# Moving the small tensors of a hybrid decoder layer behind its weight ring in SBUF

## The chip, the cores and the metric

The kernel runs on one core of a Trainium2 chip. The metric is the device time of one execution in microseconds (us), lower is better, taken as the median of the runs.

## The reference

One decoder layer on x of 1024 tokens by 1024 features, in float32, then a last RMSNorm. What matters for the work:

```python
h = rmsnorm(x, norm_mix_g)
u_pool, q, k, v, f_logit, g_logit = split(h @ w_in)            # 1024 x 4104
y_pool = pool_mixer(u_pool, pool_w, pool_scale) @ w_pool_out   # windows 2, 4, 8, 16
y_fox = forgetting_attention(q, k, v, f_logit + b_forget) @ w_fox_out   # 8 heads of 64, causal
g_pool, g_fox = split(sigmoid(g_logit + b_gate))
x = x + (g_pool * y_pool + g_fox * y_fox) @ w_out
x = x + memory_cross_attention(rmsnorm(x), rmsnorm(mem), w_xq, w_xkv, w_xo)  # 256 memory tokens
gate, up = split(rmsnorm(x) @ w_ffn_in)                        # 1024 x 5632
x = x + (silu(gate) * up) @ w_ffn_out                          # 2816 x 1024
out = rmsnorm(x, norm_final_g)
```

## The kernel before

Every matrix product is done in three passes: each operand is split into a high part in the reduced format float32r and a low part, the rest. `mm3` (lines 1553 to 1555) multiplies high by low, high by high and low by high into one PSUM bank. Weights stream from HBM in chunks of 1024 columns per partition. SyncE loads a chunk into one of two buffers `w_raw` (line 420), ScalarE copies it to one of three `w_hi` (line 657), and VectorE, or GpSimd for seven chunks, subtracts to get `w_lo` (lines 1043 and 517). TensorE waits for `w_lo`. A chunk that is a block of 128 columns of a weight arrives in pieces of 512 bytes per row of the weight; `w_pool_out` comes in pieces of 1 KB.

The stages run in this order: norm and input projections, pooling mixer, attention, gates and `w_out`, cross attention, then the FFN. Both FFN products use seven block products in place of eight (Winograd's form of Strassen's method), so GpSimd forms sums of weight blocks (`w_sum`, lines 581 to 586) and of hidden blocks (`h_sum`), and the hidden values go out to HBM (`hs_dram`) and come back into the halves of `w_raw` (line 473). Activations are split as well, on the lines 668, 984 and 1054. All engines are tied by semaphores, with the order of each engine written out by hand. Nothing in that order depends on where a tensor lies.

What the change touches is where the tensors lie in SBUF. A tensor made by `keep` stays for the whole program. The allocator gives out each partition's bytes in the order of the calls and rounds each tensor up to 32 bytes. The first `keep` tensor begins at byte 8320. A tensor made by `place(name, kb, ...)` begins kb KiB above the end of all the `keep` tensors, and such tensors overlay each other in time. Here are the `keep` tensors:

- 17 small ones for statistics, biases and counts (`ss` to `x_inv`), 1440 bytes with rounding. Most of them are read as one column of 128x1: the sum of squares `ss` (34 columns, line 506), the rsqrt `rstd`, biases.
- `w_raw`, `w_hi`, `w_lo` (eight tensors of 4096 bytes) and `ident`, `ident_r`, `mask`, `mask_r` (512 bytes each), 34,816 bytes. They are called the ring below.

Everything else (`h_hi`, `u_sb`, `win`, `z_hi`, `xr`, `hf_hi`, `wq`, `s2_hi`, `t2_hi` and so on) is placed above. Most placed tiles start a whole number of KiB above the base. The exceptions are within tiles: `u_sb` has four rows of 16 + 1024 numbers (4160 bytes a row), and `win` has 16 numbers (64 bytes) of padding in front of 1024.

Of the kernel before, what the change touches and what calls it, by code (L numbers as in the profile page):

```python
# [16 lines left out]
F32R = mybir.dt.float32r  # L17
# [4 lines left out]
P = 128  # L22
# [20 lines left out]
RAWS, SLOTS = 2, 3  # L43
# [72 lines left out]
def build(nc, x, mem, norm_mix_g, w_in, b_forget, b_gate, pool_w, pool_scale, w_pool_out,  # L116
# [12 lines left out]
    with ctx:  # L129
        def keep(name, shape, dt=FP32):  # L130
            return ctx.enter_context(nc.sbuf_tensor(name, shape, dt))
# [6 lines left out]
                return st.enter_context(nc.sbuf_tensor(name, shape, dt))  # L138


        n_tiles = N_OUT + T
        ss = keep("ss", [P, n_tiles])
        ms = keep("ms", [P, n_tiles])
# [12 lines left out]
        x_nmax = keep("x_nmax", [P, XH, T])  # L156
        x_sum = keep("x_sum", [P, XH, T])
        x_inv = keep("x_inv", [P, XH, T])

        w_raw = [keep(f"w_raw{i}", [P, 1024]) for i in range(RAWS)]  # L160
        w_hi = [keep(f"w_hi{i}", [P, 1024], F32R) for i in range(SLOTS)]
        w_lo = [keep(f"w_lo{i}", [P, 1024], F32R) for i in range(SLOTS)]
        ident = keep("ident", [P, P])
        ident_r = keep("ident_r", [P, P], F32R)
        mask = keep("mask", [P, P])
        mask_r = keep("mask_r", [P, P], F32R)


        h_hi = place("h_hi", 0, [P, KD, S], F32R)
# [1942 lines left out]
```

## Time and profile before

| | us |
|---|---|
| median of 3 runs | 1521.78 |
| lowest and highest | 1520.59, 1523.24 |
| the profiled execution's own time | 1521.78 |
| its span, first to last instruction | 1519.9 |
| outside the span | 1.9 |

Mean granted clock of TensorE: 0.990 of full speed (core 0, the only one). The span is what the profile's views explain; the 1.9 us around it are in the time alone. TensorE is abbreviated PE, its weight loads PEld, VectorE DVE, ScalarE ACT, GpSimd POOL. A group line gives the line in the kernel, the engine, the operation, what is written and read, the shapes, a count, the busy time in us and the mean duration of one in ns.

### The profile page before, as it was taken

The page shows a single profiled execution, that of the slowest core. Times are in us where ns is not written, and L with a number is a line of the kernel's source. Part 1 is how long each engine was busy: PE and PEld are TensorE (multiplying, and loading weights), DVE is VectorE, ACT ScalarE, POOL GpSimd, SP SyncE. Part 2 cuts the span into 40 slices and gives each one's busy share as a digit, 9 for nine tenths or more (in the row PEclk, how much of TensorE's full clock was granted, in tenths as well). Part 3 has the DMA queues.
Part 4 walks back from the last instruction along what each step waited for, and adds up shares of the span by engine and source line. Part 5 has one row for each costly group of instructions (what it writes and reads, how often), then busy time and mean ns, then how long its engine had stood idle before and what let it go on. Part 6 is the DMA issues. An engine that isn't in the chain of part 4 may idle for free.

```text
span 1519.9 us, 18589 instructions
## 1 busy us (share of the span) xinstructions
PE 1466.1 (96%) x7268; PEld 1211.3 (80%) x7268; DVE 898.3 (59%) x1226; ACT 555.7 (37%) x987; POOL 377.9 (25%) x311
## 2 busy tenths in 40 slices
PE   5999999999999999999999799999999999999996
PEld 5778888788787888888877678888888888887785
DVE  4272522566665423327563866777677776878966
ACT  5224311656654322216451542222222222444344
POOL 4000000000000000105001654444444443448203
PEclk9999999999999999999999899999999999999998
DMA  7333355531110352513210223323332224883333
GB/s 183 54 48 56 72 82 83 98 57 22 49 29 29 73 80 83 222 51 105 67 42 28 111 70 104 105 104 104 104 104 104 104 104 152 304 285 84 104 97 132
DMA packets 103399, 147.79 MB, mean 97 GB/s; under 512 B 4744, under 2 KB 69768, under 8 KB 101904
## 3 DMA queue, kind: packets, MB, share of 16 engines
q1 hardware_dynamic: 94288, 117.72, 30.0%
q0 software_dynamic: 4464, 15.77, 2.9%
q10 hardware_dynamic: 4560, 13.11, 2.2%
q8 instruction: 58, 0.95, 0.2%
q14 instruction: 29, 0.24, 0.1%
HBM read 113.78 MB, written 32.80 MB: 96 GB/s over the span
## 4 chain that ended last, share of the span: by engine, by line
PE 89%; DVE 5%; POOL 2%; DMA 2%; ACT 1%; issue 1%; SPq 0%; POOLq 0%; DVEq 0%; ACTq 0%
PE ps L1553 27%; PE ps L1554 27%; PE ps L1555 27%; PE ps L1803 2%; PE ps L1752 2%; PE ps L1783 1%; DMA w_raw<-in_w_in 1%; DVE t_lo L1054 1%; PE ps L1784 1%; DVE s_lo L1054 1%; POOL w_lo L517 1%; POOL rstd L509 0%; PE ps L1560 0%; PE ps L1995 0%; DVE hf_lo_B L1054 0%
## 5 line engine op out<-in xcount | busy, mean ns | idle before, releaser
L1043 DVE TENSOR_TENSOR w_lo<-w_raw,w_hi 128x1024 fp32r<-128x1024 f32 (+1 forms) x58 | 70.5, 1216 | 232.2 <-ACT w_hi L657 230.3
L1553 PE MATMUL ps<-h_lo,w_hi 128*128 128x512 f32 (+1 forms) x456 | 181.3, 398 | 6.5 <-POOL w_lo L517 4.6
L1555 PE MATMUL ps<-h_hi,w_lo 128*128 128x512 f32 (+1 forms) x456 | 176.8, 388 | 0.0
L1554 PE MATMUL ps<-h_hi,w_hi 128*128 128x512 f32 (+1 forms) x456 | 176.5, 387 | 0.0
L657 ACT ACTIVATE w_hi<-w_raw 128x1024 fp32r<-128x1024 f32 (+1 forms) x66 | 69.4, 1051 | 286.4 <-PE ps L1555 270.7
L1553 PE MATMUL ps<-t_lo,s_hi 128*128 128x512 f32 x308 | 120.2, 390 | 2.3 <-DVE t_lo L1054 1.5
L1555 PE MATMUL ps<-t_hi,s_lo 128*128 128x512 f32 x308 | 119.9, 389 | 0.0
L1554 PE MATMUL ps<-t_hi,s_hi 128*128 128x512 f32 x308 | 119.9, 389 | 0.0
L1553 PEld LDWEIGHTS ps<-h_lo,w_hi 128*128 128x128 f32 x456 | 86.4, 190 | 23.3 <-POOL w_lo L517 4.8
L1555 PEld LDWEIGHTS ps<-h_hi,w_lo 128*128 128x128 f32 x456 | 86.3, 189 | 17.8
L1554 PEld LDWEIGHTS ps<-h_hi,w_hi 128*128 128x128 f32 x456 | 86.6, 190 | 15.5
L1054 DVE TENSOR_TENSOR s_lo<-w_raw,s_hi 128x512 fp32r<-128x512 f32 x77 | 68.0, 884 | 51.4 <-ACT s_hi L984 51.4
L984 ACT ACTIVATE s_hi<-w_raw 128x512 fp32r<-128x512 f32 x77 | 48.7, 632 | 126.9 <-PE ps L1555 104.4
L1553 PE MATMUL ps<-hf_lo_T,w_hi 128*128 128x512 f32 x212 | 82.5, 389 | 0.0
L1554 PE MATMUL ps<-hf_hi_T,w_hi 128*128 128x512 f32 x212 | 82.5, 389 | 0.0
L1555 PE MATMUL ps<-hf_hi_T,w_lo 128*128 128x512 f32 x212 | 82.5, 389 | 0.0
L998 ACT ACTIVATE p_sb<-ps 128x512 f32<-128x512 f32 x22 | 13.0, 598 | 188.7 <-PE ps L1555 188.7
L1054 DVE TENSOR_TENSOR t_lo<-wq_B,t_hi 128x512 fp32r<-128x512 f32 x77 | 73.5, 954 | 0.0
L1553 PE MATMUL ps<-hf_lo_B,w_hi 128*128 128x512 f32 x164 | 66.0, 402 | 5.6 <-DVE hf_lo_B L1054 5.6
L1553 PEld LDWEIGHTS ps<-t_lo,s_hi 128*128 128x128 f32 x308 | 57.8, 188 | 16.2 <-issue 4.2
L1555 PEld LDWEIGHTS ps<-t_hi,s_lo 128*128 128x128 f32 x308 | 57.8, 188 | 12.1
L1554 PEld LDWEIGHTS ps<-t_hi,s_hi 128*128 128x128 f32 x308 | 57.8, 188 | 11.7
(303 smaller groups left out, 3658.8 us busy)
## 6 DMA issues: line engine op xcount, KB each, us to landing
w_raw<-hs_dram SPq DMA_DIRECT2D x77, 256.0 KB, 2.8
w_raw<-in_w_in SPq DMA_DIRECT2D x33, 512.0 KB, 7.7
raw_p<-in_w_ffn_in SPq DMA_DIRECT2D x22, 512.0 KB, 4.6
w_raw<-in_w_ffn_in SPq DMA_DIRECT2D x22, 512.0 KB, 4.3
hs_dram<-h_sum SPq DMA_DIRECT2D x11, 1024.0 KB, 9.0
hs_dram<-hq SPq DMA_DIRECT2D x11, 768.0 KB, 7.1
wq_B<-in_w_ffn_out SPq DMA_DIRECT2D x8, 1024.0 KB, 8.2
x_in<-in_x SPq DMA_DIRECT2D x8, 512.0 KB, 10.1
```

Source lines behind the costliest of these rows:

```text
L517: nc.gpsimd.tensor_tensor(w_lo[n % SLOTS][:], w_raw[n % RAWS][:], w_hi[n % SLOTS][:].bitcast(FP32), ALU.subtract).then_inc(lo_ready, 1)
L657: nc.scalar.activation(w_hi[n % SLOTS][:, 0:w], w_raw[n % RAWS][:, 0:w], ACT.Copy).then_inc(hi_ready, 1)
L984: nc.scalar.activation(s2_hi[n % SLOTS2][:], s_raw(n % SLOTS2), ACT.Copy).then_inc(s_split_hi, 1)
L1043: nc.vector.tensor_tensor(w_lo[n % SLOTS][:, 0:w], w_raw[n % RAWS][:, 0:w], w_hi[n % SLOTS][:, 0:w].bitcast(FP32), ALU.subtract).then_inc( ...
L1054: nc.vector.tensor_tensor(out, a, hi.bitcast(FP32), ALU.subtract).then_inc(done, 1)
L1553: nc.tensor.matmul(dst, w_h, x_l, start=start, stop=False)
L1554: nc.tensor.matmul(dst, w_h, x_h, start=False, stop=False)
L1555: return nc.tensor.matmul(dst, w_l, x_h, start=False, stop=stop)
L1752: last = nc.tensor.transpose(ps[:, 4 + g % 2, tile_of(j - j0)], prob[v % 2][:, a, tile_of(j)], ident[:])
L1783: nc.tensor.matmul(dst, q1a[:, tile_of(i)], k1a[:, keys], start=True, stop=False)
L1784: last = nc.tensor.matmul(dst, q2a[:, tile_of(i)], k1a[:, keys], start=False, stop=not diagonal)
L1803: last = nc.tensor.matmul(ps[a * DH:(a + 1) * DH, 6, 0:P], v_sb[:, j, hc:hc + DH], prob_t[:, a, tile_of(j)], start=j == 0, stop=j == v % T)
```

## The change

The small tensors are allocated after the ring and no longer before it. A tensor of 32 bytes that nothing uses (`line_fill`) is put ahead of the ring, and another (`line_fill2`) behind the small tensors. No instruction is added, removed or reordered, and no DMA changes its shape.

```diff
--- before.py
+++ after.py
@@ -138,6 +138,14 @@
                 return st.enter_context(nc.sbuf_tensor(name, shape, dt))
 
 
+        keep("line_fill", [P, 8])
+        w_raw = [keep(f"w_raw{i}", [P, 1024]) for i in range(RAWS)]
+        w_hi = [keep(f"w_hi{i}", [P, 1024], F32R) for i in range(SLOTS)]
+        w_lo = [keep(f"w_lo{i}", [P, 1024], F32R) for i in range(SLOTS)]
+        ident = keep("ident", [P, P])
+        ident_r = keep("ident_r", [P, P], F32R)
+        mask = keep("mask", [P, P])
+        mask_r = keep("mask_r", [P, P], F32R)
         n_tiles = N_OUT + T
         ss = keep("ss", [P, n_tiles])
         ms = keep("ms", [P, n_tiles])
@@ -156,14 +164,7 @@
         x_nmax = keep("x_nmax", [P, XH, T])
         x_sum = keep("x_sum", [P, XH, T])
         x_inv = keep("x_inv", [P, XH, T])
-
-        w_raw = [keep(f"w_raw{i}", [P, 1024]) for i in range(RAWS)]
-        w_hi = [keep(f"w_hi{i}", [P, 1024], F32R) for i in range(SLOTS)]
-        w_lo = [keep(f"w_lo{i}", [P, 1024], F32R) for i in range(SLOTS)]
-        ident = keep("ident", [P, P])
-        ident_r = keep("ident_r", [P, P], F32R)
-        mask = keep("mask", [P, P])
-        mask_r = keep("mask_r", [P, P], F32R)
+        keep("line_fill2", [P, 8])
 
 
         h_hi = place("h_hi", 0, [P, KD, S], F32R)
```

The addresses follow from the sizes, as the byte in each partition:

| | before | after | moved by |
|---|---|---|---|
| `line_fill` | none | 8320 | |
| small tensors, from `ss` | 8320 | 43168 | +34848 |
| ring, from `w_raw0` | 9760 | 8352 | -1408 |
| `line_fill2` | none | 44608 | |
| base of the placed tensors | 44576 | 44640 | +64 |

## Rows read from the trace of the kernel before

**Rows 1.** The page: the span, and busy time of each engine.
```profile
span 1519.9 us, 18589 instructions
...
PE 1466.1 (96%) x7268; PEld 1211.3 (80%) x7268; DVE 898.3 (59%) x1226; ACT 555.7 (37%) x987; POOL 377.9 (25%) x311
```

**Rows 2.** The page, chain that ended last: shares of the span by engine and by line.
```profile
PE 89%; DVE 5%; POOL 2%; DMA 2%; ACT 1%; issue 1%; SPq 0%; POOLq 0%; DVEq 0%; ACTq 0%
PE ps L1553 27%; PE ps L1554 27%; PE ps L1555 27%; PE ps L1803 2%; PE ps L1752 2%; PE ps L1783 1%; DMA w_raw<-in_w_in 1%; DVE t_lo L1054 1%; PE ps L1784 1%; DVE s_lo L1054 1%; POOL w_lo L517 1%; POOL rstd L509 0%; PE ps L1560 0%; PE ps L1995 0%; DVE hf_lo_B L1054 0%
```

**Rows 3.** Windows, PE alone: us, PE busy (matmuls), granted clock, DMA share, GB/s.
```profile
100.00:200.00 100.00, 100.00 (x443) 1.00 0.37 60
1000.00:1200.00 200.00, 200.00 (x884) 1.00 0.29 102
1300.00:1400.00 100.00, 100.00 (x443) 1.00 0.65 220
```

**Rows 4.** Groups by form: three matmul pairings of weights and moving tile, at 512 columns.
```profile
L1553 PE MATMUL ps<-t_lo,s_hi 128*128 128x512 f32 x308 | 120.2, 390 | 2.3 <-DVE t_lo L1054 1.5 <-issue 0.8
...
L1554 PE MATMUL ps<-hf_hi_T,w_hi 128*128 128x512 f32 x212 | 82.5, 389 | 0.0
...
L1555 PE MATMUL ps<-w_hi,z_lo 128*128 128x512 f32 x128 | 49.8, 389 | 0.0
```

**Rows 5.** VectorE adds of line 1101, 128x1024: ns min/median/max.
```profile
L1101 DVE TENSOR_TENSOR win<-win x6: 1224/1224/1226, 87.8 to 108.7; 128x1024 f32<-128x1024 f32 x6
L1101 DVE TENSOR_TENSOR win<-u_sb x4: 1219/1226/1227, 74.4 to 104.9; 128x1024 f32<-128x1024 f32 x4
```

**Rows 6.** Groups by form, VectorE, 20 to 140 us: subtraction from tiles of one residue.
```profile
L1054 DVE TENSOR_TENSOR d_lo<-pooled,d_hi 128x1024 fp32r<-128x1024 f32 x4 | 4.9, 1222 | 0.3 <-ACT d_hi L704 0.3
```

**Rows 7.** ScalarE copies from PSUM, lines 700 and 668: ns min/median/max.
```profile
L700 ACT ACTIVATE u_sb<-ps x4: 1005/1007/1010, 51.4 to 73.1; 128x1024 f32<-128x1024 f32 x4
...
L668 ACT ACTIVATE h_hi<-ps x8: 1005/1026/1028, 11.9 to 39.1; 128x1024 fp32r<-128x1024 f32 x8
```

**Rows 8.** GpSimd reads of the small tensor ss, line 506: ns min/median/max.
```profile
L506 POOL TENSOR_SCALAR ms<-ss x34: 183/191/1287, 7.6 to 1513.6; 128x1 f32<-128x1 f32 x34
```

**Rows 9.** Windows: us, PE, PEld, DVE, ACT, POOL busy (count), clock, DMA share, GB/s.
```profile
1376.00:1410.00 34.00, 32.98 (x144) 26.42 (x143) 32.77 (x24) 13.87 (x24) 34.00 (x21) 1.00 0.28 78
```

**Rows 10.** The chain from 0 to 60 us: start us, us, what.
```profile
2.69 15.62 DMA w_raw<-in_w_in
```

**Rows 11.** The chain over the whole span: two later loads.
```profile
702.70 3.70 DMA w_raw<-in_w_xkv
...
709.99 3.93 DMA w_raw<-in_w_xq
```

**Rows 12.** DMA issues: count, KB each, median us from issue to landing.
```profile
w_raw<-hs_dram SPq DMA_DIRECT2D x77, 256.0 KB, 2.8
w_raw<-in_w_in SPq DMA_DIRECT2D x33, 512.0 KB, 7.7
...
hs_dram<-h_sum SPq DMA_DIRECT2D x11, 1024.0 KB, 9.0
...
out_x<-y_out SPq DMA_DIRECT2D x8, 512.0 KB, 2.6
...
w_raw<-in_w_pool_out SPq DMA_DIRECT2D x4, 512.0 KB, 3.5
...
w_raw<-in_w_xq SPq DMA_DIRECT2D x4, 512.0 KB, 5.1
```


## The prediction, made before the kernel after was run

> **What bounds the kernel now.** I read the page first, for the busy time of each engine [rows 1]. TensorE is busy for 1466.1 of 1519.9 us. Then I read the chain that ended last [rows 2]. TensorE holds 89% of it, and 27 + 27 + 27 = 81% is the three passes of `mm3`. VectorE has 5%, DMA 2%, GpSimd 2%, ScalarE 1%. Since the chain is nearly all matmuls, the next view is how fast those run. Windows over three stages give it [rows 3]: 100 us with 443 matmuls, 200 us with 884, 100 us with 443. That is 225.7, 226.2 and 225.7 ns for each, at full granted clock. These are the input projections, the first FFN product and the second, so different pairs of tiles. The chain's 81% of 1519.9 us is 1231 us, and over 225.7 ns it is about 5450 matmuls. The groups by form say the same of the single instruction, 389 or 390 ns in each of three pairings [rows 4] (they overlap, so the rate is read from the windows). So there are two ways for this change to be felt: through the time of a matmul, 5450 times, or through the some 54 us (1519.9 - 1466.1) in which TensorE isn't busy.
>
> **The change, part by part.** It removes no instruction and no wait, and adds none. SyncE, ScalarE and GpSimd issue the same DMAs in the same order. The terms of the sum are therefore all of one kind: the same operation at another address.
>
> How far the addresses differ is in the table above. I take their remainders, because whatever a memory does by lines or banks depends on these.
>
> | start, remainder by | 64 | 128 | 256 |
> |---|---|---|---|
> | ring before, after | 32, 32 | 32, 32 | 32, 160 |
> | placed tiles before, after | 32, 32 | 32, 96 | 32, 96 |
> | `ss` before, after | 0, 32 | 0, 32 | 128, 160 |
>
> The two things to see: every large tile was off any boundary of 64 bytes by 32, and it stays off by 32. And before, ring and placed tiles had one and the same remainder even by 1024 (9760 and 44576 both leave 544), so this trace has no matmul whose weights and moving tile stand to each other as they will after: ring and placed tiles come to lie 64 bytes further apart by 128.
>
> *VectorE.* The pooling mixer is a trial inside this trace. Its sources `win[:, 16:]` leave 96 by 128 before the change, the shifted source lies 4 to 32 bytes lower, and the four rows of `u_sb` (4160 bytes each) leave 96, 160, 224 and 32 by 256. The adds took 1219 to 1227 ns [rows 5]. A subtraction whose tiles all leave 32 took 1222 on average [rows 6]. The largest difference is 8 ns of 1224, 0.7%, with both signs, and the medians 1224 and 1226 are 0.2% apart. I take 0. VectorE's 5% of the chain is 76 us, so the bounds are 0.7% of that, -0.5 and +0.5 us.
>
> *ScalarE.* The copies into the four rows of `u_sb`, at the four remainders, took 1005 to 1010 ns. The same copy into tiles that leave 32 took 1005 to 1028 [rows 7]. Again 0. With 1% of the chain, 15 us, and 23 of 1005 ns, 2.3%, as the bound it is -0.4 to +0.4 us.
>
> *The small tensors.* They are read as single columns. The 34 columns of `ss` lie 4 bytes apart, so they cover remainders 0 to 60 by 64, both halves. The median read took 191 ns and the fastest 183 [rows 8]. The maximum of 1287 is on an operation of one number and so can't be the read itself. I take 0. If each of the 34 cost 8 ns more or less in sequence, it would be 0.3 us.
>
> *GpSimd beside VectorE.* There is one stretch where VectorE sets TensorE's pace. From 1376 to 1410 us GpSimd is busy for all 34.00 us and VectorE for 32.77, and TensorE makes 144 matmuls where 34 / 0.2257 = 150.6 would fit [rows 9]. That is 1.5 us lost. If the two engines disturb each other by address, at most these 1.5 us can be won. The tiles there are nearly all placed and move together, except `w_raw`. I take 0, with bounds -1.5 and +1.5 us.
>
> *DMA.* Of no DMA does this trace show the same transfer at two remainders, so it is bounded by rows that are further off. Exposed on the chain are 15.62 us before the first weight [rows 10] and 3.70 and 3.93 us in cross attention [rows 11], 23.25 us together. The rest is covered. In the input projections a chunk is 48 matmuls, 48 x 225.7 ns = 10.8 us, and a load lands in 7.7 us [rows 12] with two buffers in hand. Without that cover, a load 10% longer would cost 0.8 us each. For the price of a badly placed piece, the nearest rows are those of piece size: 512 KB in pieces of 512 bytes (`w_xq`) took 5.1 us, in pieces of 1 KB (`w_pool_out`) 3.5 us [rows 12]. That is +46% one way and -31% the other for a factor of two in the count of pieces. On 23.25 us this makes -7.2 to +10.7 us. I take 0, since a piece that starts off a 256-byte boundary before starts off it afterwards too, and crosses as many.
>
> A rule of the Trainium skill speaks against the change here. Its page "DMA: Bandwidth & Descriptors", section "How a descriptor splits into AXI transactions", says that a transfer that doesn't start at a multiple of 256 bytes first fetches from the multiple below, in beats of 32 bytes. Counted so at the SBUF end, a 512-byte piece into the ring is 17 beats at remainder 32 and 21 at remainder 160, and an estimate by that rule is 4/17 = 24% on such pieces, up to 5.5 us on the exposed loads. The page tells it of what is fetched, and the weight loads write SBUF. For what is read from SBUF by 2 KB pieces (`h_sum`) it would be 65 to 67 beats, 3%. No row here shows either.
>
> *TensorE.* Again no row has the new relation of weights and moving tile. For the bounds, 512 columns at the 2.4 GHz of the full clock last 213.3 ns, so 12.4 ns of each 225.7 are something else. If all of it went, the gain would be 5450 x 12.4 ns = 68 us, and a second helping of it costs as much. I take 0. Pairings as different as ring weights with `h`, and `s` with `t` both placed, run at one rate [rows 3], and the two engines for which there are rows don't notice a move by 64.
>
> The sum is 0 with all terms at their values: 1519.9 us of span, 1521.8 us of time. The profiled execution's time is also the median of the three runs, so nothing has to be converted. The small terms (VectorE, ScalarE, small tensors, GpSimd) reach 2.7 us together at most.
>
> **The rivals.** By 0.2% I mean 3.0 us, about what a measurement of this kernel can tell from no change; the three runs lie within 2.65 us.
>
> - *Loads into the ring get longer (slower).* The place is the first weight chunk and the two loads of cross attention, 23.25 us [rows 10, 11]. It decides from 3.0 / 23.25 = 13% per load. Midway between nothing and the +46% of the factor of two, at 23%, it costs 5.3 us, so 1527.1. For it: ring pieces are the small ones, and they move by half of 256 bytes. Against it: the first 15.62 us also hold four tiles of x, in pieces of 4 KB that go to placed tiles, so less than half of the 23.25 us is ring loads. Then it is some 3 us, 1524.6. The skill's rule named above is this rival.
> - *Matmuls get faster (faster).* If weight loads and moving reads got in each other's way because both had one remainder, then spreading them by 64 bytes would ease it. One period of 2.4 GHz, 0.42 ns, on each of 5450 is 2.3 us, and it decides from 0.56 ns. At 1 ns it gives 5.5 us, so 1516.3. For it: the unexplained 12.4 ns. Against it: the second FFN product, where both tiles are placed, would keep its relation, and shows the same 225.7 ns as the others.
> - *Matmuls get slower by the same route.* At 1 ns 1527.3 us. Nothing speaks for it that doesn't speak for the other sign.
> - *The lines matter, and the remainders are not what I worked out.* If the true base differed from 8320 by 32 bytes, then before and after would both be on a 64-byte line together, since ring and placed tiles move by multiples of 64. The change then still does nothing to lines. Only the small tensors change half, and they are read as one number. This gives 1521.8 too and needs no chance of its own.
>
> **How the numbers follow.** No effect beyond 0.2%: 0.82. Loads or matmuls slower by more: 0.10 (0.06 and 0.04). Matmuls or loads faster by more: 0.08 (0.06 and 0.02). The predicted time is that of no effect, 1521.8 us. The small terms' 2.7 us and the runs' own spread of 2.65 us are alternatives rather than a sum, so about 3 us either way holds that case. I add a little above for the load rival at 3 us. The range is 1518.5 to 1525.5 us.
>
> **What the profile after would show.** Right: 443 matmuls in the same 100 us windows, 389 ns per form, the first weight load near 15.6 us, `u_sb` and `win` operations unchanged, `ms` reads at 190 ns. The load rival would show in the landing time of `w_raw<-in_w_in` above 7.7 us and of `w_xq` above 5.1, and in a later first matmul, with the rates behind it unchanged. The matmul rival would show 445 or more matmuls (or 441 and fewer) in 100 us of the input projections and still 443 in the second FFN product. The prediction is wrong if either the rate in those windows or the idle time of TensorE (54 us) moves by 0.2% of the span.

## The result, and the profile after

The changed kernel took 1540.4 us (median of 4 runs, 1540.08 to 1542.12), the kernel before 1521.98 us (4 runs). The ratio is 1.0124, with a 95% interval of 1.0106 to 1.0141. I had forecast no change, 1521.8 us, in a range up to 1525.5. It is 18.4 us slower, far outside the runs' spread, and the prediction was wrong.

The page of the changed kernel, its span, engines and chain (lines have moved on by one, so L1554 to L1556 are `mm3`):

```profile
span 1539.2 us, 18589 instructions
...
PE 1485.2 (96%) x7268; PEld 1210.8 (79%) x7268; DVE 899.4 (58%) x1226; ACT 557.0 (36%) x987; POOL 379.5 (25%) x311
...
PE 89%; DVE 5%; POOL 2%; DMA 2%; ACT 1%; issue 1%; SPq 0%; POOLq 0%; DVEq 0%; ACTq 0%
PE ps L1554 27%; PE ps L1556 27%; PE ps L1555 27%; PE ps L1804 2%; PE ps L1753 2%; PE ps L1784 1%; DMA w_raw<-in_w_in 1%; DVE t_lo L1055 1%; PE ps L1785 1%; DVE s_lo L1055 1%; POOL w_lo L518 1%; POOL rstd L510 0%; PE ps L1561 0%; PE ps L1996 0%; DVE hf_lo_B L1055 0%
```

Against [rows 1] the span is 19.3 us longer and TensorE's busy time 19.1 us (1485.2 against 1466.1). VectorE, ScalarE and GpSimd are within 1.6 us of before. TensorE's time without work is 54.0 us, where it was 53.8. The chain [rows 2] has the same shares. So nothing waits longer, and TensorE does the same work in more time.

Here are three windows on TensorE alone, first of the kernel before and then of the one after (us, busy and number of matmuls, granted clock, DMA share, GB/s). The first lies in the projections of the pooling mixer and the gates. The second is in the first FFN product, the third in the second.

```profile
130.00:190.00 60.00, 60.00 (x267) 1.00 0.35 67
1010.00:1190.00 180.00, 180.00 (x796) 1.00 0.31 107
1320.00:1370.00 50.00, 50.00 (x222) 1.00 0.81 279
```

```profile
130.00:190.00 60.00, 60.00 (x259) 1.00 0.36 69
1010.00:1190.00 180.00, 180.00 (x782) 1.00 0.32 110
1320.00:1370.00 50.00, 50.00 (x222) 1.00 0.90 316
```

The clock is the full one in all six. In the first window 267 matmuls became 259 (224.7 to 231.7 ns for each), in the second 796 became 782, in the third 222 stayed 222. Such a quotient is 1 to 2 ns low, since the matmuls that a window only touches are counted too: in the kernel before it is 224.7 ns from 60 us, 225.7 from 100 and 226.2 from 200. Differences between equal windows hold. The groups by form of the changed kernel tell which matmuls these are (mean ns of one behind the busy time):

```profile
L1555 PE MATMUL ps<-h_hi,w_hi 128*128 128x512 f32 x440 | 174.0, 395 | 0.0
...
L1554 PE MATMUL ps<-t_lo,s_hi 128*128 128x512 f32 x308 | 120.3, 391 | 2.3 <-DVE t_lo L1055 1.4 <-issue 0.8
...
L1555 PE MATMUL ps<-hf_hi_T,w_hi 128*128 128x512 f32 x212 | 83.8, 395 | 0.0
...
L1555 PE MATMUL ps<-hf_hi_T,late_hi 128*128 128x512 f32 x140 | 54.5, 390 | 0.0
...
L1556 PE MATMUL ps<-w_hi,z_lo 128*128 128x512 f32 x128 | 50.3, 393 | 0.0
...
L1555 PE MATMUL ps<-mt_hi,w_hi 128*128 128x256 f32 x32 | 8.8, 276 | 0.0
```

In [rows 4] three such groups stood at 389 or 390. In a group "a,b" of `mm3`, b is the 128x128 tile that is loaded into TensorE as weights, and a is the tile that is streamed past them. With weights from the ring and a placed tile streamed (`h_hi,w_hi`, `hf_hi_T,w_hi`) it is now 395. With both placed (`t_lo,s_hi` and `hf_hi_T,late_hi`) it is 390 or 391, within 1 ns of before. With the roles the other way round, placed weights and the ring streamed (`w_hi,z_lo`), it is 393, and 390 and 392 in the other two passes of `z`. One group of 256 columns (`mt_hi,w_hi`) is at 276 ns where it was 283. The second window above mixes `hf` with ring slots and with `late` slots, and so it loses less than the first.

The rest stood as forecast. VectorE's adds, the landing of loads and the first exposed load in the changed kernel:

```profile
L1102 DVE TENSOR_TENSOR win<-win x6: 1224/1226/1228, 89.1 to 110.2; 128x1024 f32<-128x1024 f32 x6
L1102 DVE TENSOR_TENSOR win<-u_sb x4: 1219/1226/1226, 75.8 to 106.4; 128x1024 f32<-128x1024 f32 x4
```

```profile
w_raw<-in_w_in SPq DMA_DIRECT2D x33, 512.0 KB, 7.7
...
w_raw<-in_w_xq SPq DMA_DIRECT2D x4, 512.0 KB, 5.0
```

```profile
2.86 16.04 DMA w_raw<-in_w_in
```

They answer to [rows 5], [rows 12] and [rows 10]: adds 1219 to 1228 ns, `w_in` 7.7 us as before, `w_xq` 5.0 for 5.1, and the first load 16.04 us for 15.62. The reads of `ss` [rows 8] have a median of 192 ns for 191.

### The profile page after: what moved, and what is told of

It is laid out like the page before. It is cut to its first block, busy times and chain, and to the rows that moved or that the text cites. A ratio compares the mean times of both kernels' runs of the same rounds, so it can differ in the third digit from the quotient of the medians.

```text
span 1539.2 us, 18589 instructions
## 1 busy us (share of the span) xinstructions
PE 1485.2 (96%) x7268; PEld 1210.8 (79%) x7268; DVE 899.4 (58%) x1226; ACT 557.0 (36%) x987; POOL 379.5 (25%) x311
## 4 chain that ended last, share of the span: by engine, by line
PE 89%; DVE 5%; POOL 2%; DMA 2%; ACT 1%; issue 1%; SPq 0%; POOLq 0%; DVEq 0%; ACTq 0%
PE ps L1554 27%; PE ps L1556 27%; PE ps L1555 27%; PE ps L1804 2%; PE ps L1753 2%; PE ps L1784 1%; DMA w_raw<-in_w_in 1%; DVE t_lo L1055 1%; PE ps L1785 1%; DVE s_lo L1055 1%; POOL w_lo L518 1%; POOL rstd L510 0%; PE ps L1561 0%; PE ps L1996 0%; DVE hf_lo_B L1055 0%
## 5 line engine op out<-in xcount | busy, mean ns | idle before, releaser
L1554 PE MATMUL ps<-h_lo,w_hi 128*128 128x512 f32 (+1 forms) x456 | 183.6, 403 | 7.1 <-POOL w_lo L518 5.2
L1556 PE MATMUL ps<-h_hi,w_lo 128*128 128x512 f32 (+1 forms) x456 | 179.0, 392 | 0.0
L1554 PE MATMUL ps<-t_lo,s_hi 128*128 128x512 f32 x308 | 120.3, 391 | 2.3 <-DVE t_lo L1055 1.4
L1556 PE MATMUL ps<-t_hi,s_lo 128*128 128x512 f32 x308 | 119.9, 389 | 0.0
L1554 PEld LDWEIGHTS ps<-h_lo,w_hi 128*128 128x128 f32 x456 | 86.5, 190 | 26.1 <-POOL w_lo L518 5.4
L1556 PEld LDWEIGHTS ps<-h_hi,w_lo 128*128 128x128 f32 x456 | 86.4, 189 | 20.1
L1554 PE MATMUL ps<-hf_lo_T,w_hi 128*128 128x512 f32 x212 | 83.8, 395 | 0.0
L1556 PE MATMUL ps<-hf_hi_T,w_lo 128*128 128x512 f32 x212 | 83.8, 395 | 0.0
L1554 PE MATMUL ps<-hf_lo_B,w_hi 128*128 128x512 f32 x164 | 66.5, 406 | 5.6 <-DVE hf_lo_B L1055 5.6
L1554 PEld LDWEIGHTS ps<-t_lo,s_hi 128*128 128x128 f32 x308 | 57.8, 188 | 16.0 <-issue 4.2
L1556 PEld LDWEIGHTS ps<-t_hi,s_lo 128*128 128x128 f32 x308 | 57.8, 188 | 12.2
```

Source lines behind the costliest of these rows:

```text
L1554: nc.tensor.matmul(dst, w_h, x_l, start=start, stop=False)
L1556: return nc.tensor.matmul(dst, w_l, x_h, start=False, stop=stop)
```

## The experiments

The kernel before was run again beside each group of experiments, and each ratio is against those runs: a median of 1522.63 us beside the first three, 1523.04 beside the bare reordering and the whole period, 1522.47 beside the distance with nothing else.

Three theories stood after that. A: what counts is the distance in SBUF between TensorE's weights and the tile that it streams, by some power of two; it was 0 by 1024 and became 192 by 256 (36288 bytes from ring to placed base). B: the ring's own remainder, 160 by 256 where it was 32. C: the new place of the small tensors. Below, "distance" is the start of the streamed tile minus the start of the weights.

**Placed tiles moved by 64 alone.**

```diff
         mask_r = keep("mask_r", [P, P], F32R)
+        keep("fill_b", [P, 16])
```

> The kernel before with 64 unused bytes between ring and placed tiles: ring and small tensors stay where they were, placed tiles move by +64. In the changed kernel a matmul with weights in the ring and a placed moving tile takes 233.4 ns from start to start where it took 226.8; with both placed it is unchanged at about 227. Theory A (what counts is the distance of weights and moving tile, by some power of two up to 512 bytes; it was 0 by 1024 and became 448 by 512): the distance is now 64, so the rate leaves 226.8 ns for ring weights, probably to about 233 (1535 to 1545 us). Theory B (the ring's own remainder by 256, 32 before and 160 after): no change, 1522 us. Theory C (the small tensors' new place): no change, 1522 us.

Measured 1536.67 us, ratio 1.0090 (1.0075 to 1.0105). With the ring and the small tensors untouched, it lost 14.0 us, three quarters of the whole. That leaves B and C at most a part. The first window falls to the changed kernel's count, and the third, with both tiles placed and both moved, does not:

```profile
130.00:190.00 60.00, 60.00 (x259) 1.00 0.37 70
1010.00:1190.00 180.00, 180.00 (x792) 1.00 0.32 110
1320.00:1370.00 50.00, 50.00 (x222) 1.00 0.89 315
```

The groups by form show more, which matters below. At this one distance of 64, ring weights with a placed tile streamed don't all run alike: `d_hi,w_hi` takes 397 ns, one more than in the changed kernel, and `hf_hi_T,w_lo` 388, one less than in the kernel before, while the same streamed tile with `w_hi` takes 394.

```profile
L1556 PE MATMUL ps<-hf_hi_T,w_lo 128*128 128x512 f32 x212 | 82.3, 388 | 0.0
...
L1555 PE MATMUL ps<-d_hi,w_hi 128*128 128x512 f32 x72 | 28.6, 397 | 0.0
```

**Ring and placed tiles moved by 128 together.**

```diff
+        keep("fill_a", [P, 32])
         w_raw = [keep(f"w_raw{i}", [P, 1024]) for i in range(RAWS)]
```

> The kernel before with 128 unused bytes ahead of the ring: ring and placed tiles move by +128 together, so the ring has remainder 160 by 256 as in the changed kernel and the distance stays 0 by 1024. Theory A: 1522 us, 226.8 ns per matmul. Theory B: slower as the changed kernel, about 1540 us. Theory C: 1522 us.

Measured 1523.48 us, ratio 1.0008 (0.9998 to 1.0017). The ring lies at the changed kernel's remainder and nothing is lost. B falls.

```profile
130.00:190.00 60.00, 60.00 (x266) 1.00 0.35 67
```

**The changed kernel with the distance put right.**

```diff
-        keep("line_fill2", [P, 8])
+        keep("line_fill2", [P, 24])
```

> The changed kernel with line_fill2 of 96 bytes in place of 32: small tensors and ring stay where the change put them, placed tiles move by +64 more, so that the distance is 0 by 512 again (512 by 1024). Theory A: back to about 1522 us if it goes by 512 or less; by 1024 it may stay slow. Theories B and C: still about 1540 us.

Measured 1524.34 us, ratio 1.0004 (0.9995 to 1.0014). The order of the change is kept whole, and 64 bytes more behind it give its loss back. C falls, and 0 by 512 is enough.

```profile
130.00:190.00 60.00, 60.00 (x266) 1.00 0.34 67
```

**Matmuls alone, by distance.** A kernel of one weight tensor `w`, one streamed tensor `m` and rows of 180 matmuls, of which each row has its own line (shortened; no layer is computed):

```python
def operands(i, a, b):
    k = i % 4
    return (ps[:, i % 8, :], w[:, a + k * P:a + (k + 1) * P],
            m[:, b + (i % 2) * HALF:b + (i % 2 + 1) * HALF])
# ...
for i in range(N):
    last = nc.tensor.matmul(*operands(i, 0, 16), start=True, stop=True)  # moving +64 B
```

> No layer is computed here: float32r matmuls of 128x128 weights with 512 columns alone, in rows of 180 with one pair of offsets each; weights and moving tile both at remainder 544 by 1024 plus the offset in the comment; moving offsets 0 to 480 in steps of 32, then both shifted by 32, weights +32 with moving +96, and moving +512, +16, +1024. Theory A: the time from start to start follows the moving offset: 226.8 ns at 0, near 233 at 448 (distance of the changed kernel), others unknown and perhaps under 226.8; +512 or +1024 as 0 if it goes by 512; both +32 as 0, weights +32 with moving +96 as moving +64. Theory B or C: all rows alike at about 227 ns.

Some of its groups, with busy us and mean ns of one. The lines are the distances 0 (L60), 32 (L62), 64 (L64), 160 (L70), 256 (L76), 448 (L88), both tensors +32 (L92) and 512 (L96):

```profile
L70 PE MATMUL ps<-m,w 128*128 128x512 f32 x180 | 42.3, 396 | 0.0
...
L62 PE MATMUL ps<-m,w 128*128 128x512 f32 x180 | 42.2, 395 | 0.0
...
L88 PE MATMUL ps<-m,w 128*128 128x512 f32 x180 | 42.2, 395 | 0.0
...
L64 PE MATMUL ps<-m,w 128*128 128x512 f32 x180 | 41.4, 391 | 0.0
...
L92 PE MATMUL ps<-m,w 128*128 128x512 f32 x180 | 41.0, 389 | 0.0
L96 PE MATMUL ps<-m,w 128*128 128x512 f32 x180 | 41.0, 389 | 0.0
...
L76 PE MATMUL ps<-m,w 128*128 128x512 f32 x180 | 41.0, 389 | 0.0
L60 PE MATMUL ps<-m,w 128*128 128x512 f32 x180 | 41.0, 389 | 0.0
```

The time from start to start is (busy - mean) / 179: for L60 (41.0 - 0.389) / 179 = 226.9 ns, for L62 and L88 233.5, for L70 234.1, for L64 229.1. The busy time has one decimal, so this is good to half a nanosecond. In these rows it goes by the distance with a period of 256 bytes. 0, 256 and 512 are alike, and 64 is a second, lesser optimum. Weights +32 with moving +96 (L94) have the 41.4 us and 391 ns of L64. Both tensors moved by 32 is as good as none, so the 64-byte line doesn't matter. It is theory A. The changed kernel's 192 is the 233 of L88 (448 = 256 + 192).

At 64 the full kernel doesn't follow this table. The first window holds 267 matmuls at distance 0 (226.9 ns alone) and 259 at 192 (233.5 alone), so 229.1 ns would make some 264. The run with 64 bytes had 259. So at 64 something besides the distance by 256 counts, and no run here shows what.

**The bare reordering, without fillers.**

```diff
-        keep("line_fill", [P, 8])
...
-        keep("line_fill2", [P, 8])
```

> The changed kernel without its two fillers: the bare reordering. Ring from 8320, placed tiles from 44576, so both are on 64-byte lines of their own kind (ring 0, placed 32 by 64) and the distance from ring to placed tiles is 160 by 256, back 96. By the table of the matmuls alone (period 256 bytes; 226.7 ns at distance 0, 228.9 at 64, 234.3 at 160, about 233.3 at the other steps of 32) some 3050 matmuls with ring weights and a placed moving tile cost 7.6 ns more and some 770 with the roles changed 6.7 ns: 23 + 5 = 28 us, of which a few may be hidden. Theory A: 1544 to 1551 us, slower than the changed kernel. Theory D (the fillers themselves, or being 32 past a 64-byte line, cause the loss): about 1522 us.

Measured 1545.34 us, ratio 1.0157 (1.0136 to 1.0178), inside the range that theory A had worked out from the lone matmuls, and the slowest of all. D, which puts the loss on the fillers or on the ring's 32 bytes past a 64-byte line, falls: here are no fillers, and the ring begins on such a line.

```profile
130.00:190.00 60.00, 60.00 (x258) 1.00 0.36 69
1010.00:1190.00 180.00, 180.00 (x780) 1.00 0.30 102
```

**A whole period.** In the kernel before:

```diff
         mask_r = keep("mask_r", [P, P], F32R)
+        keep("fill_b", [P, 64])
```

> The kernel before with 256 unused bytes between ring and placed tiles (the run with 64 gave 1536.7 us). Theory A with a period of 256 bytes: 1522 us. With a period of 512 or 1024: slower, above 1530 us.

Measured 1522.39 us, ratio 0.9996 (0.9987 to 1.0005). The period is 256 in the full kernel as well.

```profile
130.00:190.00 60.00, 60.00 (x267) 1.00 0.34 67
```

**The changed kernel's distance with nothing else of it.** In the kernel before:

```diff
         mask_r = keep("mask_r", [P, P], F32R)
+        keep("fill_b", [P, 48])
```

> The kernel before with 192 unused bytes between ring and placed tiles. Ring and small tensors lie where they lay before; only the distance from ring to placed tiles is that of the changed kernel, 192 by 256 (back 64). Theory A: the whole loss of the changed kernel, 1538 to 1542 us, 233.4 ns with ring weights and placed moving tile. If the small tensors' place or the ring's own remainder had any part in the loss: clearly less, with the rest missing.

Measured 1541.15 us, ratio 1.0116 (1.0099 to 1.0133), against 1.0124 for the change. These two windows have the very counts of the changed kernel:

```profile
130.00:190.00 60.00, 60.00 (x259) 1.00 0.36 69
1010.00:1190.00 180.00, 180.00 (x782) 1.00 0.31 109
```

**Finer distances, and which weights count.** As the lone matmuls above, rows of 150. The two rows that ask whose weights count are

```python
last = nc.tensor.matmul(*operands(i, 32 * (i % 2), 32 * (i % 2)), start=True, stop=True)        # L94
last = nc.tensor.matmul(*operands(i, 32 * (i % 2), 32 * ((i + 1) % 2)), start=True, stop=True)  # L96
```

> Matmuls alone again (no layer), 150 per row, 512 columns. First the moving tile at finer distances (4, 8, 16, 24, 40, 48, 56, 72, 80, 112, 144, 176, 208, 240, 248, 252 bytes): if a place exists that is better than distance 0 it shows under 226.7 ns. Then rows whose weights alternate by 128 or 64 bytes: moving tile at distance 0 to the weights it meets, or to the weights of the next matmul. If the moving read of one matmul is disturbed by the weight load of the next, the rows with distance 0 to the next weights take 226.7 ns and the others 233 (128 B); if a matmul's own weights count, the other way round.

L60 is distance 0, L62 4 bytes, L88 240 bytes. L94 has distance 0 to its own weights and 128 to the next, L96 the other way round:

```profile
L62 PE MATMUL ps<-m,w 128*128 128x512 f32 x150 | 35.7, 399 | 0.0
...
L96 PE MATMUL ps<-m,w 128*128 128x512 f32 x150 | 34.7, 392 | 0.0
...
L94 PE MATMUL ps<-m,w 128*128 128x512 f32 x150 | 34.4, 390 | 0.0
L60 PE MATMUL ps<-m,w 128*128 128x512 f32 x150 | 34.2, 389 | 0.0
L88 PE MATMUL ps<-m,w 128*128 128x512 f32 x150 | 34.2, 388 | 0.0
```

By (busy - mean) / 149 it is 226.9 ns at 0, 236.9 at 4 and 226.9 at 240. No distance was better than 0. The two rows that were to tell whose weights count gave 228.3 and 230.3 ns, between the two levels expected. A second pair with 64 in place of 128 bytes gave 231.6 ns with 0 to its own weights (L98, 34.9 us, 394 ns) and 233.6 with 0 to the next (L100, 35.2 us, 396 ns). In both pairs 0 to its own weights is the faster by 2 ns, but neither reaches 226.9, so this stays open: in them the weights of successive matmuls lie at two different remainders, and that was not separated.

**Other widths.** Rows of 240 with 256 and with 128 columns.

```diff
-            m[:, b + (i % 2) * HALF:b + (i % 2 + 1) * HALF])
+            m[:, b + (i % 2) * HALF:b + (i % 2) * HALF + cols])
```

> Matmuls alone (no layer), 240 per row, with 256 and then 128 columns, moving tile at distances 0 to 224 in steps of 32. In the changed kernel 256-column matmuls with ring weights and the memory tokens as moving tile went from 124.8 to 119.0 ns at distance 192: so at 256 columns distance 192 should be near 119 and 0 near 125. At 128 columns the weight load (188 ns record) may set the pace: then all alike.

L60 and L72 are 256 columns at distance 0 and 192, L76 and L84 128 columns at 0 and 128:

```profile
L60 PE MATMUL ps<-m,w 128*128 128x256 f32 x240 | 29.0, 283 | 0.0
...
L72 PE MATMUL ps<-m,w 128*128 128x256 f32 x240 | 27.4, 276 | 0.0
L84 PE MATMUL ps<-m,w 128*128 128x128 f32 x240 | 27.0, 275 | 0.0
...
L76 PE MATMUL ps<-m,w 128*128 128x128 f32 x240 | 26.9, 274 | 0.0
```

At 256 columns 192 is the better distance, (27.4 - 0.276) / 239 = 113.5 ns against 120.2. The direction of `mt_hi,w_hi` was as expected, and the durations 283 and 276 are those of the full kernel. The expected 125 and 119 were too high. Why the full kernel's matmuls of this form start further apart than these isn't shown. At 128 columns the distance does nothing.

**Narrower weights.** Rows of 150 with 512 columns.

```diff
-    return (ps[:, i % 8, :], w[:, a + k * P:a + (k + 1) * P],
+    return (ps[0:wide, i % 8, :], w[:, a + k * step:a + k * step + wide],
```

> Matmuls alone (no layer), 150 per row, 512 columns. Weights of 128, 64 and 32 columns, moving tile at distance 0, 64, 128, 160, 192; then both shifted by 64, 128, 160 at distance 0 and 192; then one weight tile again and again. If the loss is the weight load disturbing the read of the moving tile, it shrinks with the columns of the weights: at 32 columns all distances near 213.3 ns (512 columns at 2.4 GHz) plus little. If it has to do with the moving read alone, the loss is the same for all widths. Shifted rows: 226.7 and 233.3 ns whatever the shift, if only the distance counts.

L66 is 160 bytes with 128 weight columns, L70 and L72 64 weight columns at distance 0 and 64, L80 and L86 32 weight columns at distance 0 and 160, L98 and L100 both tensors +160 at distance 0 and 192, L102 and L104 one weight tile again and again at 0 and 128:

```profile
L66 PE MATMUL ps<-m,w 128*128 128x512 f32 x150 | 35.3, 396 | 0.0
...
L104 PE MATMUL ps<-m,w 128*128 128x512 f32 x150 | 35.2, 395 | 0.0
...
L100 PE MATMUL ps<-m,w 128*128 128x512 f32 x150 | 35.2, 394 | 0.0
...
L80 PE MATMUL ps<-m,w 128*32 128x512 f32 x150 | 34.9, 394 | 0.0
...
L86 PE MATMUL ps<-m,w 128*32 128x512 f32 x150 | 34.8, 393 | 0.0
L70 PE MATMUL ps<-m,w 128*64 128x512 f32 x150 | 34.7, 392 | 0.0
...
L72 PE MATMUL ps<-m,w 128*64 128x512 f32 x150 | 34.4, 391 | 0.0
...
L102 PE MATMUL ps<-m,w 128*128 128x512 f32 x150 | 34.2, 389 | 0.0
L98 PE MATMUL ps<-m,w 128*128 128x512 f32 x150 | 34.2, 389 | 0.0
```

With 128 weight columns, a distance of 0 (L98) gives (34.2 - 0.389) / 149 = 226.9 ns and 160 gives 234.3. With 64 weight columns the best of the five distances is 64 and not 0: 228.3 ns against 230.3, and the slowest, 192, takes 232.9. With 32 weight columns 0 and 160 give 231.6 and 230.9. So the spread shrinks with the width of the weights, from 7.4 ns over 4.6 to about 1, and the best distance changes with it. But the level does not go to 213.3 ns as expected. At 32 weight columns it is near 231 at every distance. That part of the expectation fell. One weight tile again and again (L102, L104) behaves as four in turn do, 226.9 ns at 0 and 233.6 at 128.

## Why the prediction was wrong

Right were the reading of the chain (TensorE's rate is what can be felt), the addresses, and the terms of VectorE, ScalarE, the small tensors, the loads and GpSimd. All of them together would show in TensorE's time without work, and that grew by 0.2 us. The rival of longer loads didn't happen. The Trainium skill's rule ("DMA: Bandwidth & Descriptors", "How a descriptor splits into AXI transactions") had been weighed for it. The estimate by that rule was 24% more on the ring's pieces. They landed in 7.7 us for 7.7 and 5.0 for 5.1, so for writes into SBUF this trace doesn't bear it out. The test named at the end was right too: in 100 to 200 us, the first window of [rows 3], 443 matmuls became 432, and in the 50 us of the second FFN product above the number stayed.

The step that failed is the term of TensorE, "I take 0". It gave two reasons. The first, that pairings as different as ring with `h` and `s` with `t` run at one rate, was no evidence. The prediction itself had noted that all of them had one remainder by 1024. They were one case measured several times. The second, that VectorE and ScalarE don't notice a move by 64, is true and doesn't carry over to TensorE, which loads weights while it streams a tile: the two were busy for 1211.3 and 1466.1 us of 1519.9 [rows 1]. The bounds (68 us both ways) held the effect, but the rival of slower matmuls had 0.04 and a price of 1 ns, where 6.6 was measured. It was also set beside the faster one as if distance 0 were no special place. All tiles stood at it.

The size follows from the lone matmuls. In the groups of the kernel before, ring weights with a placed tile streamed make 3 x (440 + 212 + 164 + 72 + 64 + 64) = 3048 matmuls of 512 columns (`h`, `hf_T`, `hf_B`, `d`, `o`, `hx`), and placed weights with the ring streamed 3 x (128 + 64 + 64) = 768 (`z`, `h`, `xo`). From ring to placed tile the distance is 192, and 233.5 - 226.9 = 6.6 ns make 20.1 us. From placed to ring it is 64, and 2.2 ns make 1.7 us. The 96 of 256 columns, each 7 ns shorter, give back 0.7. The sum is 21.1 us against 19.1 more busy time and 19.3 more span, 10% too much. The same way the bare reordering had been put at 28 us over, where 22.3 were measured (1545.34 against 1523.04). The run with 64 bytes comes out the other way: 3048 x 2.2 + 768 x 6.6 ns make 11.8 us, where 14.0 were measured, because at 64 some pairings run slower than the lone matmuls.

The groups by form show where the changed kernel's sum is too large. The three `hf_B` groups with ring weights grew by 1.6 us (196.7 to 198.3), where 3 x 164 x 6.6 ns make 3.2. They also ran at a better clock: from 840 to 920 us the granted clock was 0.91 before and 0.94 after. So part of what the address cost there was given back by the clock. That is no effect of the address: the three runs with a filler and a distance of 0 by 256 have 0.94 as well. The three `h` groups grew by 7.1 us (519.0 to 526.1), where 3 x 440 x 6.6 ns make 8.7. Attention, where projections are mixed with small matmuls, is the likely place of that; it was not measured.

Shown is this: the loss of this change comes with the distance alone (192 bytes of filler give all of it, 64 bytes more in the changed kernel give it back), distances of 0, 256 and 512 are alike in the full kernel, and the effect depends on the width of the weights. Not shown is the mechanism. That the weight load and the streamed read disturb each other fits the smaller spread of narrow weights, but not their flat 231 ns. Why pairings differ at 64, and whether a matmul's own or the next one's weights count is open. Also open is why 226.9 ns remains at the best distance, where the prediction reckoned with 213.3 for 512 columns. No version faster than the kernel before came out. Its distance of 0 is already the best one found for 128x128 weights with 512 columns.

## What to carry to other kernels

If float32r matmuls of 128x128 weights with 512 columns bound the kernel, keep the distance in bytes between the weight tile and the streamed tile at a multiple of 256, and look at it after every reordering or added tensor: here distances of 64, 192 and 160 bytes cost 0.9, 1.2 and 1.6%. For 256 columns or narrower weights another distance was the best, so measure it for the shape at hand. When one resource has the same setting everywhere in a trace, the trace says nothing about another setting, however many rows agree. Then weigh the unknown by what it can cost, and a setting that looks chosen deserves a rival that it is the good one.

## What the runs showed of the hardware that was not expected

- Alone, float32r matmuls of 128x128 weights with 512 streamed columns start every 226.9 ns at a distance of 0 or 240 bytes by 256, every 229.1 at 64, every 233.5 at 32 or 192, 234.1 at 160, and 236.9 at 4, all at full granted clock. In the full kernel 192 gives the same, but in the first window 64 ran like 192 (259 matmuls in 60 us).
- With 256 columns, 192 is better than 0 (113.5 against 120.2 ns). With 128 columns nothing depends on it (111.4 and 111.8).
- Moving both tensors together changes nothing, and nor does being 32 bytes off a 64-byte boundary. The durations of the weight loads don't show the effect (PEld is busy for 1210.8 us, 1211.3 before).
